# Moving the gate operand by 48 elements, and four spare matmuls ahead of chunk 3, in a hybrid decoder layer

## The reference

```python
xn = rms_norm(h, attn_norm)
qm, km, vm, qs, ks_, vs = split(xn @ w_in, 6)
h = h + concat(rms(moba(qm, km, vm)), rms(stick_breaking(qs, ks_, vs))) @ w_out
h = h + peer_ffn(rms_norm(h, ffn_norm))
h = h + sigmoid(rms_norm(h, ple_norm) @ w_gate) * (p @ w_ple)
```

## Time and profile before

| | |
|---|---|
| median of 3 runs | 945.83 us |
| the runs | 945.51, 945.83, 950.56 us |
| profiled execution, its own time | 949.53 us |
| its span, first to last instruction | 947.8 us |
| PE busy | 940.5 us (99%) |
| DVE, ACT, POOL busy | 688.2, 615.4, 333.8 us |
| mean granted clock of PE | 1.000 |

### The profile page before, as it was taken

The page is one execution under the profiler, slowest core; times in us unless marked ns, Lnnn a source line. Parts: engine busy times, 40 slices in busy tenths (PEclk is TensorE's granted clock), DMA queues, the critical chain, the costliest instruction groups (busy, mean ns, idle before and its releaser), DMA issues.

```text
span 947.8 us, 19175 instructions
## 1 busy us (share of the span) xinstructions
PE 940.5 (99%) x6220; PEld 858.1 (91%) x6220; DVE 688.2 (73%) x1389; ACT 615.4 (65%) x1039; POOL 333.8 (35%) x148
## 2 busy tenths in 40 slices
PE   9999999999999999999999999999999999999998
PEld 6988889999999999999999998888888888888887
DVE  6658864999987888888988865555555555566663
ACT  7678754556676888888888875445545445456643
POOL 0003500388887777777777781000000000000000
PEclk9999999999999999999999999999999999999999
DMA  9860453055555454544445455555567776555521
GB/s 341 320 241 1 174 208 124 24 183 192 179 187 179 168 177 158 176 162 170 160 172 170 162 178 189 190 198 193 186 240 242 230 256 224 189 188 199 185 103 45
DMA packets 46459, 172.08 MB, mean 182 GB/s; under 512 B 5043, under 2 KB 8668, under 8 KB 44892
## 3 DMA queue, kind: packets, MB, share of 16 engines
q1 hardware_dynamic: 46284, 171.53, 52.2%
q10 hardware_dynamic: 144, 0.15, 0.1%
HBM read 169.55 MB, written 2.11 MB: 181 GB/s over the span
## 4 chain that ended last, share of the span: by engine, by line
PE 91%; ACT 3%; DVE 2%; issue 2%; POOL 1%; DMA 0%; DVEq 0%; POOLq 0%; ACTq 0%
PE bank L1264 12%; PE bank L1265 12%; PE bank L1266 12%; PE pair L1600 12%; PE pair L1602 12%; PE pair L1603 12%; PE pair L1561 3%; PE pair L1299 1%; PE pair L1301 1%; PE pair L1300 1%; PE bank L1299 1%; PE bank L1301 1%; PE bank L1300 1%; PE bank L1645 1%; PE bank L1643 1%
## 5 line engine op out<-in xcount | busy, mean ns | idle before, releaser
L616 ACT ACTIVATE t_hi<-t_raw 128x1024 fp32r<-128x1024 f32 x256 | 270.3, 1056 | 166.7 <-DMA t_raw<-v_chunks 162.2
L1236 POOL TENSOR_TENSOR t_lo<-t_raw,t_hi 128x1024 fp32r<-128x1024 f32 x130 | 311.5, 2408 | 142.6 <-ACT t_hi L616 142.4
L1264 PE MATMUL bank<-xt_hi,t_hi 128*128 128x256 f32 x1024 | 286.5, 280 | 0.2 <-POOL t_lo L1236 0.2
L1265 PE MATMUL bank<-xt_lo,t_hi 128*128 128x256 f32 x1024 | 286.0, 279 | 0.0
L1266 PE MATMUL bank<-xt_hi,t_lo 128*128 128x256 f32 x1024 | 285.9, 279 | 0.0
L967 DVE TENSOR_TENSOR t_lo<-t_raw,t_hi 128x1024 fp32r<-128x1024 f32 x126 | 154.4, 1225 | 136.8 <-ACT t_hi L616 136.4
L1600 PE MATMUL pair<-t_hi,g_hi 128*128 128x512 f32 x512 | 199.5, 390 | 0.2 <-DVE g_lo L1147 0.2
L1602 PE MATMUL pair<-t_lo,g_hi 128*128 128x512 f32 x512 | 199.2, 389 | 0.0
L1603 PE MATMUL pair<-t_hi,g_lo 128*128 128x512 f32 x512 | 199.2, 389 | 0.0
L1264 PEld LDWEIGHTS bank<-xt_hi,t_hi 128*128 128x128 f32 x1024 | 193.5, 189 | 0.4 <-POOL t_lo L1236 0.4
L1266 PEld LDWEIGHTS bank<-xt_hi,t_lo 128*128 128x128 f32 x1024 | 193.6, 189 | 0.0
(11 more groups left out here) (285 smaller groups left out, 1283.6 us busy)
## 6 DMA issues: line engine op xcount, KB each, us to landing
t_raw<-u_chunks SPq DMA_DIRECT2D x128, 512.0 KB, 3.2
t_raw<-v_chunks SPq DMA_DIRECT2D x128, 512.0 KB, 3.3
w_raw<-w_query SPq DMA_DIRECT2D x4, 2048.0 KB, 7.9
w_raw<-w_in SPq DMA_DIRECT2D x3, 2048.0 KB, 10.5
w_raw<-w_out SPq DMA_DIRECT2D x2, 2048.0 KB, 8.2
wg_raw<-w_gate SPq DMA_DIRECT2D x8, 512.0 KB, 5.1
first_raw<-first SPq DMA_DIRECT2D x7, 384.0 KB, 6.1
w_raw<-w_in SPq DMA_DIRECT2D x4, 512.0 KB, 9.6
```

Of the source, the lines that this page charges most:

```text
L616: nc.scalar.activation(t_hi[:, q % RING, :], t_raw[:, q % RING, :], ACT.Copy).then_inc(t_hi_ready, 1)
L1236: nc.gpsimd.tensor_tensor(t_lo[:, q, :], t_raw[:, q, :], t_hi[:, q, :].bitcast(f32), ALU.subtract).then_inc(t_lo_pool, 1)
L1264: mm(dst, ah, bh, start=(c == 0), stop=False)
L1265: mm(dst, ah, bl, start=False, stop=False)
```

## The change

Offsets change: `hot_j` moves by 48 elements (`HI_AT`). It then reaches 48 elements further, so `t_hi` and all that lies behind it, BIG's tiles too, move by 64. And chunk 3 gets four more matmuls, behind its waits and ahead of its own 24. They multiply 128 columns of `t_hi` with the 256 behind them and write the PSUM half that chunk 3's first matmul then starts anew, so no result uses them.

```diff
-        BIG = ZONE + 4 * 13312
+        BIG = ZONE + 4 * 13376
...
-        hot_j = tile("hot_j", [P, 2, 4, 2, P], ZONE + 4 * 5120, f32r)
+        hot_j = tile("hot_j", [P, 2, 4, 2, P], ZONE + 4 * (5120 + HI_AT), f32r)
...
-        t_hi = tile("t_hi", [P, RING, D], ZONE + 4 * 7168, f32r)
-        o = ZONE + 4 * 11264
+        t_hi = tile("t_hi", [P, RING, D], ZONE + 4 * 7232, f32r)
+        o = ZONE + 4 * 11328
         pick_t = tile("pick_t", [P, 3, SEQ], o); o += 4 * 768
...
-        low = tile("low", [P, 2, 4, P], ZONE + 4 * 12032)
-        gate_hi = tile("gate_hi", [P, SEQ], ZONE + 4 * 12032, f32r)
-        gate_lo = tile("gate_lo", [P, SEQ], ZONE + 4 * 12288)
+        low = tile("low", [P, 2, 4, P], ZONE + 4 * 12096)
+        gate_hi = tile("gate_hi", [P, SEQ], ZONE + 4 * 12096, f32r)
+        gate_lo = tile("gate_lo", [P, SEQ], ZONE + 4 * 12352)
...
                 if q == RING - 1:
                     pe.wait_ge(gelu_done, q - 1)
+                    for _ in range(4):
+                        mm(hid_bank(q), t_hi[:, q, 0:P], t_hi[:, q, P:P + SEQ], start=True, stop=True)
                 else:
                     pe.wait_ge(s_out, q + 1)
                 hidden(q)
```

## The result

The changed kernel takes 954.27 us, the median of 22 runs (947.83 to 955.90); the kernel before 946.60 us in 22 runs beside them (945.35 to 950.56). The ratio, formed within each set of runs side by side, is 1.0061 with a 95% interval of 1.0049 to 1.0074: slower by 0.6%, clear of the noise. The forecast was 940. Of the cases, D, "both slow", gave 954.6, and had a chance of 0.05.

The account below looks back on a forecast made before the run. TensorE's pace through its own instructions was taken as the bound; -6.3 (late stretch fast), -3.5 (chunks 3 to 35 fast) and +0.47 (spares) gave -9.3 from 949.53, so 940.2 us, said as 940; 8-in-10 range 936.5 to 951.

Parts of the forecast that it names:

- D: Chunks 3 to 35 and the late stretch both slow, needing spares that act one way only: 954.6 us (950.9); chance 0.05.
- all-slow late stretch: Chunks 36 to 127 with their gate matmuls, 2464 at 117.8 ns: 290.2 us against 285.65, a loss of 4.6.
- The move's mechanism: Gate matmuls at the chunks' own spacing no longer flip the pitch; late stretch in one state, 6.3 us gained if fast.
- Rival E: Gate sets still flip the pitch after the move, late half stays mixed: 946.5 us, or up to 950; chance 0.18.
- waiting did not flip it: At chunk 2, TensorE stood for POOL at 188.73 us and resumed at the slow pitch, 117.9 ns; one case.
- The second base of the prediction: Counting from the runs' median, 945.83 us, 3.7 below the profiled 949.53; perhaps lower runs found chunks 2 to 35 fast.
- the transposes set the stream to fast: The six transposes at 284.94 us, ahead of chunk 36, leave the fast pitch; all-fast late stretch gains 6.3 us.
- case A: Both stretches fast, from chunk 3 and after the transposes: 940.2 us (936.5 on the median's base); chance 0.35.
- B: Chunk 2 resumes fast, spares make chunks 3 to 35 slow, transposes make the rest fast: 943.7 us (940.0); chance 0.20.
- each group of other matmuls flips the pitch: Between two stretches of 256-column matmuls, each group of others turned slow to fast or back, 117.8 against 113.3 ns.
- the argument from Q_S: Query group, unshifted operands: 120.0 ns a matmul with xt_hi and xt_lo, 64 modulo 128 apart, so spacing counts modulo 64.
- the zero for the V stage: 512-column matmuls reading t_hi: operands a multiple of 64 apart before and after, so 0 us from the move by 64.

Follow-up runs that it names:

- e1: The changed kernel without the four spare matmuls, only the move of hot_j: 948.78 us, ratio 1.0018 to the kernel before.
- e5: The kernel before with one, two, three or five spares at spacing 0 ahead of chunks 4 to 39, by place in the ring: 960.46 us, one run.
- e11: The kernel before with g_hi and g_lo 48 elements further, so V-stage spacing is 16 modulo 64: 953.03 us, one run.
- e2: The kernel before with the four spare matmuls added at chunk 3, nothing moved: 950.36 us, ratio 1.0032.
- e4: The changed kernel with what lies between hot_j and BIG, t_hi included, moved by 128 elements instead of 64: 954.49 us, ratio 1.0065.
- e7: The kernel before with g_hi and g_lo 16 elements further, so V-stage spacing is 48 modulo 64: 959.83 us, ratio 1.0127.
- e10: The kernel before with g_hi and g_lo 32 elements further, so V-stage spacing is 32 modulo 64: 955.27 us, one run.
- e12: The changed kernel with five spare matmuls at chunk 3 in place of four: 949.70 us, ratio 1.0027.
- e3: The changed kernel with the four spares taken from chunk 3 and put behind the transposes, ahead of chunk 36: 949.62 us, ratio 1.0031.
- e8: e4's layout without spares, three matmuls of each gate set at spacing 0 and the fourth at 48: 942.69 us, ratio 0.9963 to the kernel before.
- e9: e8 with five spare matmuls ahead of chunk 3: 942.55 us, ratio 0.9958 to the kernel before.

## Why the prediction was wrong

*The reading of the kernel was right.* PE's pitch sets the end, there is a fast and a slow one with the same instructions, and no engine or wait took part. An all-slow late stretch was put at 290.2 us and measured 290.29; the spares at 0.47 and measured 0.46.

*The move's mechanism was right.* Gate sets at 48 leave the pitch as it is: 64 sets slow in the changed kernel, nine sets fast in e1. Rival E falls with it. With t_hi moved by 64 the chunks of e1 still run at the fast pitch, so the shift does not slow a stream by itself.

*The step that failed: the state in which each stretch starts.* It failed in three places. First, "waiting did not flip it ... that is one case". It was the exception: chunk 2 resumed slow in the profile before, slow again in those of e5 and e11, and fast in the other eleven. So in most runs four spares did not rescue a slow stretch but spoiled a fast one; e2 shows that price alone (950.4 against 946.3). The second base of the prediction, that the lower runs find chunks 2 to 35 fast, fits all of this (no lower run of the kernel before was profiled), and I gave the sum to the other. Second, that the transposes set the stream to fast. From slow they left fast (before, e2, e11) and slow (after, e4); from fast they left fast (e1, e7 to e10, e12). The three that went from slow to fast have the old addresses and the two that stayed slow the moved ones, and e2 and the changed kernel differ in nothing else up to there: same spares, same late load. So the move may have a part in the slow late stretch besides the gate sets; five traces, and no run separates it from chance. Third, and not seen at all: the fast pitch does not last. In e1, e3 and e12 it ended at chunk 53, at a stall of about 0.015 us, and at spacing 48 nothing brought it back. So even a fast start, e1's and e12's, lost the last 75 chunks, and no run of either came near case A, 940.2 (the lowest are 944.10 and 945.03 us). Gate sets with matmuls at spacing 0 look like a cost of half the chunks, but such a set can also end a slow stretch: in the kernel before each one flips the pitch, and in e8 and e9 the next one restored the fast pitch after each slow chunk.

*How the loss adds up.* Against a typical run before, with chunks 3 to 35 fast: 3.5 for these chunks, 0.5 for the spares, 4.6 for the late stretch. That is 8.6 us; the medians differ by 7.7, of runs in two clusters on either side. The prediction took 0.5 off for a kernel before that reaches the transposes fast, as its chunks 36 to 40 would be slow; e7 and e10, the kernel before up to the V stage, did reach them fast, and their late stretch is 285.65 us all the same.

*Luck in a number.* D gave 954.6 and the runs 954.27, and both stretches are slow in the profile, as D says. But D asked for spares that act in one direction only, and they don't: chunk 2 resumed fast and the spares made it slow, as in B. No case of the prediction joined that to a slow late stretch.

*Two rules too simple.* That each group of other matmuls flips the pitch holds for an even number at spacing 0; an odd one kept a fast stream fast (e5, e12), though five also turned a slow one fast (e5). And the argument from Q_S, 120.0 ns at spacing 0, does not carry over to 512 columns, where spacing 0 is best (e7); the zero for the V stage held (its matmuls span 349.60 us before and 348.98 after) because nothing moved modulo 64, not because spacing is harmless there. What the prediction drew from the Trainium skill's two independent read ports (TensorE: Matmul & The Clock Gate, Step-by-step: what each phase is for), that operand spacing changes nothing, stays contradicted: e7 changes nothing but the addresses of g_hi and g_lo and pays 6.7 ns in each matmul.

*What stays open.* The lower cluster of the changed kernel, 947.8 to 950.4 us, was not caught in a profile; that chunk 2 resumed slow there and the spares made it fast is argued only. Why the transposes leave one state or the other, and whether the move has a part in it, what the hiccups are, and whether a distance or one operand's own address sets the pitch are open too. 4.6 us of the loss hang on the state that the transposes left.

## What to carry to other kernels

Where a stream of equal matmuls has two pitches, an edit that takes away what flips them makes one state last, and one must ask which, and how long the good one lasts: better something cheap that keeps the good state and leads back to it. Here that was an odd number of spacing-0 matmuls in each gate set (e8, 3.6 us faster by the medians) instead of an even one. And one profile shows one start: the spread of the runs told already that the profiled execution was the rarer kind, and the sum belonged on the other base.

## What the runs showed of the hardware that I had not expected

A shift of one operand by 64 bytes (16 elements) changes a matmul's pitch at a granted clock of 1.00: 226.7, 233.3, 232.5 and 229.2 ns with 512 columns, the weights shifted by 0, 16, 32 and 48 elements (before, e7, e10, e11; spacing 0, 48, 32 and 16). With 256 columns and the moving operand shifted by 48 it is 113.3 or 117.8 ns instead of 120.0. Both 113.3 and 117.8 ns last for hundreds of matmuls of the same code. In three traces the first ended for good at a stall of about 0.015 us, and elsewhere it outlived stalls of 28 to 39 ns. A few matmuls at spacing 0 in a fast stream keep it fast if they are one, three or five, and make it slow if they are two or four.
